# Softmax scaling moved from the probabilities into the matrix that turns them, in two attention stages of an fp32 two-block kernel

## What is computed

```
# latent attention: 8 heads, 512 queries, 768 keys, head size 192, value size 128
s = einsum('bqhd,bkhd->bhqk', qblk, k) * scale
p = softmax(s, axis=-1)
o = einsum('bhqk,bkhv->bqhv', p, v)

# banded attention with a sink, both layers of the second block: 8 heads of 64, blocks of 128 queries
m = maximum(max(scores), sink)
p = exp(scores - m)
p = p / (sum(p) + exp(sink - m))
out = einsum('bnhgqk,bnkhd->bnqhgd', p, v)
```

## Time and profile before

| | us |
|---|---|
| three runs | 2878.43, 2878.53, 2878.58 |
| median | 2878.53 |
| the profiled execution, whole | 2879.39 |
| its span, first to last instruction | 2877.6 |
| latent attention | 1108 to 1239 |
| banded attention, two layers | 1704 to 1802, 2318 to 2417 |

### The profile page before, as it was taken

How to read it: one execution, slowest core, us unless ns; L and a number is a source line. 1 busy time by engine, 2 the same in 40 slices (tenths; PEclk the granted TensorE clock), 3 DMA queues, 4 the chain that set the end, 5 groups by cost and what they waited for, 6 DMA issues and landing times.

```text
span 2877.6 us, 36797 instructions
## 1 busy us (share of the span) xinstructions
PE 2825.0 (98%) x14214; PEld 2366.2 (82%) x14214; DVE 1738.6 (60%) x2633; ACT 1208.8 (42%) x1842; POOL 59.0 (2%) x115
## 2 busy tenths in 40 slices
PE   8999999999999999999999999999999999999999
PEld 6998899999999966788888876578888765688887
DVE  5846758754674454447546468865365488855463
ACT  4235644321333384445334345653233455643231
POOL 0000000000000000000000010000000010000000
PEclk9999999999999999999999999999999999999999
DMA  7720023333432120022323231122223321123223
GB/s 286 232 91 29 1 92 125 126 129 104 131 122 71 59 75 15 1 77 96 102 89 102 89 113 62 32 85 98 93 97 103 105 80 45 52 95 105 86 100 106
DMA packets 73485, 266.16 MB, mean 92 GB/s; under 512 B 8816, under 2 KB 11376, under 8 KB 72032
## 3 DMA queue, kind: packets, MB, share of 16 engines
q1 hardware_dynamic: 63360, 230.31, 24.1%
q0 software_dynamic: 9952, 33.50, 3.4%
HBM read 253.55 MB, written 2.10 MB: 89 GB/s over the span
## 4 chain that ended last, share of the span: by engine, by line
PE 87%; DVE 6%; issue 4%; ACT 3%; DMA 0%; SPq 0%; ACTq 0%; DVEq 0%
PE psum L746 73%; DVE arena L1933 2%; ACT temps L1390 2%; DVE row_stats L1933 2%; PE psum L1118 2%; PE psum L1335 1%; PE psum L1273 1%; PE psum L1126 1%; PE psum L1146 1%; PE psum L840 1%; PE psum L841 1%; PE psum L839 1%; ACT arena L1390 1%; DVE temps L1933 1%; PE psum L1255 0%
## 5 line engine op out<-in xcount | busy, mean ns | idle before, releaser
L746 PE MATMUL psum<-arena_r,w_hi 128*128 128x512 f32 (+1 forms) x7416 | 2006.0, 369 | 2.9 <-DVE arena_r L1933 2.2
L746 PEld LDWEIGHTS psum<-arena_r,w_hi 128*128 128x128 f32 x7416 | 1337.7, 188 | 221.5 <-issue 61.5
L746 PE MATMUL psum<-arena_r,w_lo 128*128 128x512 f32 (+1 forms) x3708 | 1219.6, 364 | 0.0
L1933 DVE TENSOR_TENSOR w_lo<-w_raw,w_hi 128x1024 fp32r<-128x1024 f32 (+4 forms) x377 | 455.5, 1208 | 523.3 <-ACT w_hi L1390 522.4
L746 PEld LDWEIGHTS psum<-arena_r,w_lo 128*128 128x128 f32 x3708 | 682.8, 188 | 82.5
L1390 ACT ACTIVATE w_hi<-w_raw 128x1024 fp32r<-128x1024 f32 (+4 forms) x377 | 392.7, 1042 | 539.6 <-DMA w_raw<-in_weights 539.4
L1390 ACT ACTIVATE temps<-temps 128x512 f32<-128x512 f32 (+2 forms) x202 | 132.2, 657 | 152.1 <-DVE temps L1933 149.9
L1933 DVE SCALAR_TENSOR_TENSOR temps<-psum,vectors,temps 128x511 f32<-128x511 f32 x246 | 151.0, 656 | 62.8 <-ACT temps L1390 60.9
L1390 ACT ACTIVATE arena<-psum 128x768 f32<-128x768 f32 (+1 forms) x144 | 101.6, 711 | 190.6 <-PE psum L746 61.6
L1390 ACT ACTIVATE arena_r<-temps 128x512 fp32r<-128x512 f32 (+1 forms) x103 | 70.7, 686 | 142.4 <-DVE temps L1933 142.4
L1933 DVE TENSOR_TENSOR arena_r<-temps,arena_r 128x512 fp32r<-128x512 f32 (+1 forms) x103 | 78.2, 759 | 78.7 <-ACT arena_r L1390 78.7
(11 more groups left out here) (212 smaller groups left out, 2285.4 us busy)
## 6 DMA issues: line engine op xcount, KB each, us to landing
w_raw<-in_weights SPq DMA_DIRECT2D x261, 512.0 KB, 3.3
w_raw<-in_weights SPq DMA_DIRECT2D x64, 704.0 KB, 4.1
arena<-in_ada SPq DMA_DIRECT2D x32, 512.0 KB, 3.6
arena<-in_ada POOLq DMA_DIRECT2D x24, 512.0 KB, 4.7
modulation_weights<-in_ada POOLq DMA_DIRECT2D x24, 512.0 KB, 3.8
arena<-in_ada_first SPq DMA_DIRECT2D x8, 1024.0 KB, 19.2
w_raw<-in_weights SPq DMA_DIRECT2D x32, 256.0 KB, 2.6
modulation_weights<-arena POOLq DMA_DIRECT2D x60, 128.0 KB, 1.9
```

The costliest lines, as they stand in the source:

```text
L746: last = mm(lin_at(t, segs, slots, upper)[:, s:s + m], w[:, c], x(k, s, m), start=(k == 0 and a == 0), stop=(k == n_k - 1 and a == 2))
L1933: op(*args, **kw).then_inc(*C.out(signal))
```

## The change

In both attentions the exponentials stay unscaled. DVE still makes the reciprocals, but then multiplies the 128x128 identity by them, which gives a diagonal matrix: one for a latent block (in a buffer of `temps` that the stage does not use otherwise), two for a banded block, one for each head (in the unused tail of the block's own 1024 columns). `turn` multiplies each piece of the exponentials with that diagonal by a plain product in place of the transpose: exp^T times diag(1/sum) is the transposed, scaled piece. Counts of semaphores between engines stay the same.

```
+        def latent_diagonal(n):
+            return T[:, 0, n % 4 * P:n % 4 * P + P]
+
+        def band_diagonal(n, hf):
+            return f_(E2 + n % 4 * 1024 + 768 + hf * P, P)

 # turn, latent
-                    last = pe.transpose(flat(0)[:, t * P:(t + 1) * P], E1[n % 4][:, t * P:(t + 1) * P], ident)
+                    last = mm(flat(0)[:, t * P:(t + 1) * P], E1[n % 4][:, t * P:(t + 1) * P], latent_diagonal(n), start=True, stop=True)

 # turn, banded
-                            last = pe.transpose(PS[:, 6 + hf, t * P:(t + 1) * P], f_(a, P), ident)
+                            last = mm(PS[:, 6 + hf, t * P:(t + 1) * P], f_(a, P), band_diagonal(n, hf), start=True, stop=True)

 # probs, latent
-                step(ts, "p_made", E1[n % 4], E1[n % 4], ST[:, 16 * b + 3:16 * b + 4], None, ALU.mult, after=C.at("dve_own"))
+                step(ts, "p_made", latent_diagonal(n), CF[:, C_ID:C_ID + P], ST[:, 16 * b + 3:16 * b + 4], None, ALU.mult, after=C.at("dve_own"))

 # probs, banded
-                    step(tt, "p_made", e, e, ST[:, s + 12:s + 14].rearrange("p (h o) -> p h o", o=1).broadcast_to([P, 2, w]), ALU.mult,
-                         after=C.at("dve_own"))
+                    known = C.at("dve_own")
+                    for hf in range(2):
+                        step(ts, "p_made" if hf else "dve_own", band_diagonal(n, hf), CF[:, C_ID:C_ID + P], ST[:, s + 12 + hf:s + 13 + hf],
+                             None, ALU.mult, after=known)
```

## The result

| | before | after |
|---|---|---|
| median of the runs on one chip, us | 2878.48 (2878.25 to 2878.58) | 2898.44 (2897.85 to 2899.67) |
| the profiled execution, us | 2879.39 | 2898.03 |
| its span, us | 2877.6 | 2896.2 |

The change costs 20.0 us: the ratio of after to before is 1.0071, with a 95% interval of 1.0059 to 1.0083. 2900.2 was predicted, in a range of 2896.5 to 2908. Lines of the functions touched stand 6 further down after the change: 1136 is 1142, 1146 is 1152, 1240 is 1246, and DVE's helper is on 1939.

A forecast was written before the change was run, and what follows sets the result against it. PE was taken as the bound in both stages, its queue growing by the added records less its idle time: 16.8 us latent plus 4.9 banded, 21.7 in all, giving a median of 2900.2 us, range 2896.5 to 2908.

The forecast's parts named there:

- The price of a piece: PE's turns in both attentions: a plain fp32 product takes two records, 0.223 us, against 0.109 for a transpose, 0.114 more.
- Rival 1: Banded turns, line 1240: a diagonal product costs one record, 0.109 us, so the kernel gets faster, 2869.5 us; 3%.
- rival 3: Turns in both stages: a plain product costs four transposes, 0.436 us a piece, about 95 us more, 2974 us; 2%.
- Latent attention, 16.8 predicted: PE's queue in latent attention: 21.9 us added less waits of 0.7, 3.8 and 0.7 leaves 16.8 us.
- the cover: Added PE work in latent attention falling into old waits: 0.7 at the first turn, 13 x 0.29, 0.7 at the end.
- Latent attention on DVE: DVE's product shrinks from 0.621 to 0.29 us, saving 0.33 us a block, worth nothing on the path.
- The banded stages, 2.5 a layer predicted: PE's queue in each banded stage: 9.1 us added less 6.6 of real idle time, 4.9 us in two layers.
- PE is the bound in the band, by a tenth: In a banded four-block period PE arrives 0.64 us later, DVE's diagonal is ready 0.56 later, so PE sets the end.
- Rival 2: Banded stages: the waits at turns stay because DVE is late; in full 35.1 us, 2913.6; 7% for anything over 2908.
- the prediction's walk: Following PE and DVE through one banded period of four blocks, 24.2 us: the period becomes 24.84 us without DVE waits at turns.
- firm floor: Whole kernel: the added records less all idle time, 21.7 us; at most 3 to 4 us lower.

The follow-up runs named there:

- e3: Kernel before with plain products by the fixed identity in both stages, DVE still scaling the exponentials: 2903.56 us, ratio 1.0087.
- e10: Kernel before with three of six pieces in latent attention's even-block turns multiplied plainly by the identity: 2877.52 us in one run.
- e4: Kernel before with DVE making the diagonals but PE still transposing with the identity, so the scaling is left out: 2870.09 us, ratio 0.9971.
- e7: e3 with ACT's exponentials of the next banded block queued ahead of the copy of the turned block: 2903.07 us, ratio 1.0089 to the kernel before.
- e6: e5 with the change's diagonal and plain products at the banded turns of query block 1 only: 2871.79 us, ratio 0.9981 to the kernel before.
- e5: Kernel before with DVE's banded product made per head as two TENSOR_SCALARs instead of one TENSOR_TENSOR, transposes kept: 2874.51 us, ratio 0.9988.

## Why the prediction was right

Its numbers come from the length of PE's queue less the idle time in it, and both were right to a few tenths.

- **The price of a piece.** Two records, 0.223 us against 0.109: confirmed by the counts of lines 1142 and 1246, and by e3, where PE's part alone makes all of the 16.02 us. Rival 1 (the price of a transpose) would have shown one record a piece and rival 3 (four transposes) 2974 us; neither happened. By the Trainium skill, "TensorE: Matmul & The Clock Gate", section "Terms", transpose mode should be four times faster for FP32; the traces before and after have a factor of 2.05, and the 16.0 us leave no room for another. The rule of the Trainium skill in "Perfetto Trace Analysis", section "Transposes", that a logical transpose should be a transpose, is borne out by e3, where the same transposes as plain products cost 25.5 us; with DVE's part added, the change still cost 20.
- **Latent attention, 16.8 predicted, 16.04 measured.** The term that was mis-sized is the cover: 21.9 us were added and 5.9 taken up, where the prediction had 0.7 + 13 x 0.29 + 0.7 = 5.1. A pair takes 9.63 us and not 9.69. e10 shows that a pair can take up at least 0.34. I had counted the idle time up to the start of `plain` and not the slower start behind it. The starts within a pair show it all: the idle 0.29 before `plain` is gone, and so is the 0.10 behind it; against them, the turn behind `rotated` grew by 0.73 and not by 0.685, from 0.71 (1167.46 to 1168.17) to 1.44 (1162.87 to 1164.31), where the other turn now takes 1.34. 0.29 + 0.10 - 0.045 = 0.345, and 13 of these with twice 0.685 make the 5.9.

```profile
1162.87 1.60 PE L1142 MATMUL psum<-temps 128*128 128x128 f32 x12
1164.31 1.50 PE L1152 MATMUL psum<-arena 128*128 128x128 f32 x12
1165.65 1.46 PE L1124 MATMUL psum<-arena 128*128 128x512 f32 x4
1166.94 1.50 PE L1142 MATMUL psum<-temps 128*128 128x128 f32 x12
1168.28 1.50 PE L1152 MATMUL psum<-arena 128*128 128x128 f32 x12
1169.62 1.46 PE L1124 MATMUL psum<-arena 128*128 128x512 f32 x4
```

This is the pair of the earlier trace rows after the change; the wait of 0.32 ahead of `plain` is not there. One wait of this kind is left in the stage, the first, with 0.7 us (the waits of the window of that stage: total us, times, longest):

```profile
PE psum L1124 <- ACT temps L1396: 0.7, 1, 0.7
```

It was 1.47 in the earlier trace rows, so the first turn's 0.7 us went into it, as predicted. At the end of the stage the same happened: 0.2 us are left of the 0.92 at line 1136, and now ACT is named there (the row of line 1142 above).

- **Latent attention on DVE.** Nothing on the path: e4's 0.00. Its busy time in the stage fell from 59.6 to 49.6 us, the 10 that were predicted. The estimate of 0.29 us for a diagonal was 0.286.
- **The banded stages, 2.5 a layer predicted, 2.15 and 2.21 measured.** 9.1 us were added and 6.9 taken up, where the prediction had 6.6. By the starts, the idle time ahead of the turns gave 5.06 us in the first layer and that ahead of the value products 1.62, together 6.7. Three turns that no longer wait gave 0.05 each; the rest is that a piece costs 0.113 rather than 0.114. The period is 24.81 us (1761.70 to 1786.51), predicted 24.84.
- **PE is the bound in the band, by a tenth.** The timeline shows how close that was:

```profile
1761.11 0.49 DVE L1939 TENSOR_SCALAR arena<-fixed_constants,row_stats 128x128 f32<-128x128 f32 x2
...
1761.64 1.42 PEld L1246 LDWEIGHTS psum<-arena 128*128 128x128 f32 x12 [0.21 <-DVE arena L1939]
1761.70 1.55 PE L1246 MATMUL psum<-arena 128*128 128x128 f32 x12
```

The two diagonals are over after 0.49 us (0.50 predicted) at 1761.60, and the turn starts at 1761.70, the weight load having waited for them. It is nearly a tie, and it came out as the prediction's walk had it: no wait on PE itself. The late weight load is not quite free, though: this turn takes 1.31 us up to the next product (1763.01), where one whose load does not wait takes 1.26 (1780.12 to 1781.38). Rival 2 (the waits stay) did not come, but e3 shows what stood behind it: without DVE's part there are 1.7 us of waits at four turns and 5.1 us a layer. What the prediction's walk did not hold is ACT's copy in front of the exponentials, which e7 found. It made no difference to the change, since PE sets the pace there: the chain of the stage is PE's alone.
- **The sum.** 21.7 predicted, 20.4 measured by the stages and 20.0 by the medians. The prediction called 21.7 a firm floor, the added records less all the idle time there is. The floor was not firm: most of the difference is time that the waits cost beyond the idle time itself, above all the slower `plain` behind its wait, 13 x 0.10 less 13 x 0.045. The range allowed for it; the sum did not have it.

## What to carry to other kernels

When an engine is full, price an edit by the length of its queue, piece by piece in the records of the trace, and subtract only idle time that stands on its own path. Work taken from an engine with time to spare is worth nothing where it has no one waiting (latent attention), and where it has, it is worth what it takes off the waits (4.0 us a layer in e4). A trick that moves work from the waited-for engine to the full one pays where a wait long enough to hold the added work follows in the full engine's queue (e6), and not everywhere: look for a cheaper form on the waited-for engine first (e5).

## What the runs showed that I had not expected

- Behind its wait `plain` loses some 0.10 us more than the idle time in front of it: 1.39 us from `plain` to the next turn with the wait, 1.30 without it (e10), 1.29 (the change). A banded turn loses 0.05. In both, the weight load starts with the product when there is a wait, and 0.11 (`plain`) or 0.23 us (the turn) ahead of it when there is none; no run tests whether that is the reason.
- The first twelve-record turn behind `rotated`, whose products have 64 rows, takes 1.44 us and the same turn behind `plain` 1.34.
- A TENSOR_SCALAR whose scalar is one value per partition took 0.351 us at 256 columns (e6), 0.418 at 384, 0.487 at 512 and 0.621 at 768, where the TENSOR_TENSOR with the broadcast reciprocal took 0.692 and 0.958 at 512 and 768. Two short ones in a row are cheaper than one TENSOR_TENSOR, although they have two starts.
- The first 400 us of the program, with the same instructions, differ by up to 2.2 us from run to run, which is a third of what the best kernel here gained. The shift of starts over a stage is the measure that told the kernels apart.
